# Transposed attention probabilities in the score banks, regrouped attention steps, and three loads moved into the projection

## The chip, the cores and the metric

The kernel runs on one core of a Trainium2 chip. The time is device microseconds of that core for one execution of the whole program, lower is better. Engines: PE multiplies matrices (PEld loads its weights, beside it), DVE, ACT and POOL work on vectors, and SP here only issues transfers. PE writes its results to eight PSUM banks of 128 x 512 float32; ACT and DVE read them from there.

## What is computed

One layer of a hybrid decoder: 2048 tokens of width 1024, all in float32. The parts that matter here are the projection and the two mixers.

```python
proj = h @ w_in[l]
# heads A: causal attention, 8 heads, query blocks of 128 tokens
s = einsum('bqhd,bkhd->bhqk', qn, k_nope) + einsum('bqhr,bkr->bhqk', qp, k_pe)
s = where(k_pos <= q_pos, s * scale, -inf)
p = softmax(s, axis=-1)
o = einsum('bhqk,bkhd->bqhd', p, v)
# heads B: gated delta rule, a recurrence over chunks of tokens, 4 heads
v_new = u_c - einsum('bhcd,bhde->bhce', w_c, state)
o_c = einsum('bhcd,bhde->bhce', q_c, state) + einsum('bhcs,bhse->bhce', a_c, v_new)
state = state * exp(g_last) + einsum('bhcd,bhce->bhde', kd_c, v_new)
x = x + gate_a * (concat([y_mla, y_gdn]) @ w_out[l])
```

After that come a second norm, a mixture of experts and a final norm; neither is touched.

## The kernel before, in words

The program is a row of parts with a barrier between them. `projection` (L73) makes keys, queries, values and the delta rule's inputs, 16 tiles of 128 tokens, and stores them to scratch tensors in HBM (`kn_d`, `kp_d`, `v_d`, `qkv_d`, `g_d`). `mix` (L806) loads them again and runs both mixers at once. `output`, `routing`, `experts` and `finish` follow.

Within a part each engine runs one list of instructions in order, and semaphores keep the engines apart. In `projection` the list `order` (L77) is written out by hand; SP runs through it and issues a store wherever a step has one (L227 to L261).

In `mix` the list comes from a planner, `mix_order` (L707). It has two streams. The delta stream is a fixed row of steps for each chunk of 128 tokens (K and KA make products of keys, VT and KD transpose, KS and QS read the state, TR, DS and AV update it, Y and WU combine inverted blocks, I is a piece of POOL's inversion, M a piece of the modulation). The attention stream is cut into 80 units, called quads: a quad is a query tile, four heads and up to four key tiles (its width, 1 to 4), and its steps are

- S: eight score matmuls into four banks of their own, `pS[0..3]`, one for each head (L1453 to L1468). It waits until all four exponentials of the quad before are done.
- X, for each of four heads: DVE takes the row minimum of the score bank (L1321, or L1318 with the mask), ACT takes the exponential into `prob` in SBUF (L1212).
- T, for each of four heads: up to four PE transposes of `prob` (L1469 to L1474) into a bank taken from a pool of three that all delta steps share, then a copy to `probT` in SBUF, by ACT for heads 0 and 2 (L1218), by DVE for heads 1 and 3 (L1326).
- V, for each of two head pairs: the products with the values (L1475 to L1488), and a copy of them by ACT (L1224).
- O, A, AS, B, BX, B2: the parts of a query tile are weighted and put together.

The eight banks are so: four for scores, one for V's output (`pO`), three in the pool (`NBANK`, L811). The planner hands the pool out in the order of the steps (L894 to L913): a step that takes a bank waits on PE until the last reader of that bank is done (L1372). K and KS take two of the three.

Each attention step has a cost in the planner, and a step is put in when the delta steps so far have earned it: `atoms.append((0.13 * n, [("T", j, e)]))` says that each T costs 0.13 per key tile, so delta steps may stand between one T and the next. The delta steps cost 0 to 1.0, and one unit of them earns a fixed number of attention units, so that both streams end together.

At the start of `mix` SP issues its first loads in this order (L1018 to L1031): `kqv` of chunk 0, g of chunk 0, queries of tile 0 (two), the first four tiles of keys (four transfers of `kp_d`, one of `kn_d`), `kqv` and g of chunk 1, values of the first four tiles, and more. PE's first steps are K of chunk 0 and 1 and S of quad 0. DVE can't write K's second product before the first has been stored to `a_d`, and POOL's inversion starts when both have been stored and loaded back (`load_blocks`, L962).

## Time and profile before

| | |
|---|---|
| median of 3 runs | 2556.26 us (2554.1 to 2560.18) |
| the profiled execution | 2557.7 us, its span 2556.0 us |
| PE busy | 2246.4 us, 88% |
| mean granted PE clock | 0.939 |
| projection | to about 690 us |
| mix | about 691 to 1598 us |
| output and after | to 2556 us |

How to read it: times in the trace are microseconds from the start of the span. A PE row's duration is stretched where the granted clock is low, so PE's busy time holds both work and lost clock; idle PE time stands in brackets before the row that ended it, with what released it. Rows of the same kind that touch are merged and counted (x8).

### The profile page before, as it was taken

Reading aid. Unit: us, or ns where it says so; the run is one execution under the profiler, and the core shown is the slowest. Engines: PE = TensorE matmul, PEld = TensorE weight load, DVE = VectorE, ACT = ScalarE, POOL = GpSimd, SP = SyncE. Lnnn points to the kernel's source line nnn. Section 1 sums busy time; section 2 is a strip of 40 time slices with the busy share of each in tenths; the row PEclk is TensorE's granted clock in tenths of the full one; section 3 lists DMA queues with packets and bytes.
Section 4 is the critical chain, followed back from the end, with each engine's and each line's share of the span. In section 5 each row is a group of like instructions: output and inputs, shape, how many; then the busy total and the mean of one; then the engine's idle time right before and its main releaser. Section 6 shows DMA issues by size and latency. Waiting matters only on the chain. (4 is left out here: it accounts for less than half of the span.)

```text
span 2556.0 us, 35821 instructions
## 1 busy us (share of the span) xinstructions
PE 2246.4 (88%) x11478; PEld 1261.6 (49%) x11479; DVE 1034.5 (40%) x2278; ACT 842.9 (33%) x2027; POOL 644.9 (25%) x1119
## 2 busy tenths in 40 slices
PE   6999999999777888888889888799975999999990
PEld 2545545455344555556555565355543444444440
DVE  2434334333344565556556565223444222222223
ACT  2263462633643444444444454111110101010112
POOL 1000000000152532524514420223321222222224
PEclk9999999999887999899989999799987999999995
DMA  9112121111343234324323224733321879999787
GB/s 346 68 62 71 52 79 54 52 54 36 127 147 106 69 108 162 88 80 134 93 96 113 84 71 168 254 120 132 118 80 42 238 204 303 278 323 308 219 237 287
DMA packets 221899, 361.79 MB, mean 142 GB/s; under 512 B 45580, under 2 KB 143527, under 8 KB 218295
## 3 DMA queue, kind: packets, MB, share of 16 engines
q1 hardware_dynamic: 207926, 309.57, 35.5%
q0 software_dynamic: 13824, 50.34, 8.1%
q8 instruction: 82, 1.34, 0.2%
q14 instruction: 67, 0.54, 0.1%
HBM read 259.93 MB, written 99.93 MB: 141 GB/s over the span
## 5 line engine op out<-in xcount | busy, mean ns | idle before, releaser
L687 PE MATMUL pV<-mod_rows_then_work,w_in_sb 128*128 128x512 f32 x768 | 340.1, 596 | 4.1 <-DVE mod_rows_then_work L501 4.1
L2118 PE MATMUL hidden_ps<-w,keys_values_then_all 128*128 x752 | 332.3, 595 | 0.1
L1212 ACT ACTIVATE probs<-scores,neg_max 128x512 f32<-128x512 f32 (+3 forms) x320 | 198.6, 624 | 337.5 <-DVE neg_max L1321 216.1
L1473 PE MATMUL bank<-ident,probs 128*128 128x128 f32 x1088 | 181.4, 299 | 112.3 <-ACT probs_T L1218 68.2
L2118 PEld LDWEIGHTS hidden_ps<-w,keys_values_then_all 128*128 128x128 f32 x752 | 143.5, 191 | 181.1 <-issue 181.0
L687 PEld LDWEIGHTS pV<-mod_rows_then_work,w_in_sb 128*128 128x128 f32 x768 | 144.4, 191 | 177.0 <-issue 176.2
L1767 PE MATMUL out_ps<-keys_values_then_all 128*128 128x512 f32 x512 | 227.3, 602 | 2.5 <-ACT keys_values_then_all L1632 2.5
L1473 PEld LDWEIGHTS bank<-ident,probs 128*128 128x128 f32 x1088 | 126.2, 149 | 156.9 <-ACT probs_T L1218 84.1
L2128 PE MATMUL expert_ps<-w_sb,keys_values_then_all 128*128 x368 | 169.8, 604 | 0.0
L2048 ACT ACTIVATE keys_values_then_all<-hidden_ps 128x256 f32<-128x256 f32 x47 | 18.1, 385 | 455.3 <-PE hidden_ps L2118 455.3
L1767 PEld LDWEIGHTS out_ps<-keys_values_then_all 128*128 128x128 f32 x512 | 97.4, 193 | 122.7 <-issue 117.4
L1326 DVE COPY probs_T<-bank 128x512 f32<-128x512 f32 (+3 forms) x160 | 97.4, 609 | 142.8 <-PE bank L1473 142.2
L1321 DVE TENSOR_REDUCE neg_max<-scores 128x1 f32<-128x512 f32 x192 | 122.7, 684 | 74.1 <-PE scores L1465 73.6
L1465 PE MATMUL scores<-keys_values_then_all,queries 64*128 64x512 f32 (+3 forms) x640 | 150.6, 593 | 0.0
L1125 POOL TENSOR_TENSOR keys_values_then_all<-keys_values_then_all 32x31 f32<-32x31 f32 (+15 forms) x248 | 121.0, 488 | 115.5 <-DMA keys_values_then_all<-a_d 95.6
L1486 PE MATMUL outT_ps<-probs_T,keys_values_then_all 128*64 128x128 f32 x2176 | 146.9, 282 | 0.0
L1127 POOL TENSOR_TENSOR keys_values_then_all<-keys_values_then_all 32x31 f32<-32x31 f32 (+15 forms) x248 | 133.2, 537 | 19.4
L1486 PEld LDWEIGHTS outT_ps<-probs_T,keys_values_then_all 128*64 128x64 f32 x2176 | 119.8, 139 | 36.5 <-issue 32.8
L2077 DVE TENSOR_TENSOR keys_values_then_all<-keys_values_then_all,hidden_ps 128x256 f32<-128x256 f32 x47 | 19.8, 421 | 277.2 <-ACT keys_values_then_all L2048 277.2
L2013 POOL DMA_INDIRECT x_d<-keys_values_then_all,out_row x46 | 73.3, 1594 | 185.9 <-DVE keys_values_then_all L2086 173.0
L2086 DVE SCALAR_TENSOR_TENSOR keys_values_then_all<-expert_ps,slot_gate,keys_values_then_all 128x512 f32<-128x512 f32 x92 | 64.8, 747 | 133.1 <-PE expert_ps L2128 133.1
L632 PE MATMUL pG<-w_in_sb,mod_rows_then_work 128*128 128x512 f32 x256 | 114.5, 601 | 0.0
(355 smaller groups left out, 3233.1 us busy)
## 6 DMA issues: line engine op xcount, KB each, us to landing
w<-in_w_dram SPq DMA_DIRECT2D x64, 1024.0 KB
w_sb<-in_w_dram SPq DMA_DIRECT2D x32, 1024.0 KB
w_mod_rows<-in_w_mod_dram SPq DMA_DIRECT2D x16, 1024.0 KB, 4.8
kqv<-qkv_d SPq DMA_DIRECT2D x16, 768.0 KB, 4.9
mod_rows_then_work<-in_w_mod_dram SPq DMA_DIRECT2D x4, 2048.0 KB, 14.9
x_in<-in_x_dram SPq DMA_DIRECT2D x16, 512.0 KB, 5.1
qkv_d<-l_out SPq DMA_DIRECT2D x32, 256.0 KB, 2.3
keys_values_then_all<-y_d SPq DMA_DIRECT2D x16, 512.0 KB, 4.7
```

The costliest lines, as they stand in the source:

```text
L632: last = pe.matmul(pG[:], hT[:, n // ST % 2, k, n % ST * P:(n % ST + 1) * P], win[:, k, GATE0:GATE0 + GH * GD], start=(k == 0), stop=(k == ...
L687: last = pe.matmul(pV[n % 2][:], win[:, k, QKV0 + c * P:QKV0 + (c + 1) * P], hT[:, s % 2, k, :], start=(k == 0), stop=(k == ND - 1))
L1125: then(pool.tensor_tensor(prod, Ab[:, j, j + 1:].unsqueeze(2).to_broadcast([n, below, upto]), Tb[:, j:j + 1, 0:upto].to_broadcast([n, belo ...
L1127: then(pool.tensor_tensor(Tb[:, j + 1:, 0:upto], Tb[:, j + 1:, 0:upto], prod, ALU.subtract))
L1212: act.activation(prob[:, e, 0:w].rearrange("p t k -> p (t k)"), pS[e][:, 0:w * P], ACT.Exp, scale=-1.0, bias=nmin[:, i % 2, h, b:b + 1], a ...
L1321: dve.tensor_reduce(nmin[:, i % 2, h, b:b + 1], pS[e][:, 0:w], AX.X, ALU.min).then_inc(min_ready, 1)
L1465: last = pe.matmul(pS[e][:, 0:w * P], qN[row64[e % 2], i % 2, hp], kN[row64[e % 2], 4 * b:4 * b + w, hp], start=False, stop=True)
L1473: last = pe.transpose(bank[b0][:, t], prob[:, e, t], m.ident[:])
L1486: last = pe.matmul(pO[64 * e:64 * e + 64, step[2]], v[:, 4 * b + t, h * DV:(h + 1) * DV], probT[:, 2 * step[2] + e, t], start=(t == 0), st ...
L1767: last = pe.matmul(pX[:, half], yT[par][:, k], wo[:, k, half * 512:(half + 1) * 512], start=(k == 0), stop=(k == ND - 1))
L2118: last = pe.matmul(pH[par][:], xT[par][:, k], m.w13[:, ds(slot, 1), k].rearrange("p s n -> p (s n)"), start=(k == 0), stop=(k == ND - 1))
L2128: last = pe.matmul(pY[:, half], hT[par][:, k], m.w2b[:, ds(slot, 1), k, half * 512:(half + 1) * 512].rearrange("p s n -> p (s n)"), start= ...
```

## The change

Four things change.

1. The transposes of head e go into `pS[e]`, the bank from which its exponential was just read, and the copies read from there. T leaves the list of steps that take a bank from the pool (`uses`). S of the next quad no longer waits for the exponentials but for the copies of the quad before (`t_copied`, both halves).
2. The planner's attention steps are grouped otherwise: T of heads 0 and 1 are one piece with 0.2 per key tile, T of heads 2 and 3 one piece with 0.05, then the O steps, then S with 0.8 (was 0.66), then V of both pairs and X of heads 2 and 3 as one piece with 0.65, in the order V, X, X, V (was V, X, V, X in two pieces). The sum is as before, 1.7. The small steps A and AS move ahead of the last V for some tiles.
3. The first four key tiles, the first four value tiles and `kqv` of chunk 0 are loaded near the end of the projection: SP issues them (seven transfers) after the HQ step of tile 13. The three groups of loads are gone from the start of `mix`.
4. For that the big buffer `m.kv` is allocated before the projection, which works inside it: its rows, weights and scratch are laid out there so that the places of the first keys, values and `kqv` are free by then. The rows for the decay move from half 0 to half 1 of `x_in`, with a wait for one more tile. Keys lie in four segments (`KEYS`) with two views each.

```diff
-        big = sb("mod_rows_then_work", [P, 2, ND, D])
-        flat = big[:].rearrange("p a k n -> p (a k n)")
+        flat = m.kv[:, 0:KV_W]
+        space = Arena(m.kv, (KV_W, KV_N))
         mod_rows = flat.rearrange("p (k n) -> p k n", k=ND)
         QKV0, GATE0 = LOWW, LOWW + NC * P
-        wuq, wukv = sb("w_uq_sb", [P, 2, AH * QK]), sb("w_ukv_sb", [P, AH * (NOPE + DV)])
-        xin, xn = sb("x_in", [P, 2, D]), sb("x_normed", [P, D])
+        xn, xin = space([P, D]), space([P, 2, D])
+        wuq, wukv = space([P, 2, AH * QK]), space([P, AH * (NOPE + DV)])
...
-        gate = sb("gate_out", [P, GH * GD])
+        gate = space([P, GH * GD])
...
-        alog, dtb = xin[:, 0, 0:GH], xin[:, 0, GH:2 * GH]
-        xs, absx, bcl, alpha = (xin[:, 0, at:at + NT * GH] for at in (64, 128, 192, 256))
+        alog, dtb = xin[:, 1, 0:GH], xin[:, 1, GH:2 * GH]
+        xs, absx, bcl, alpha = (xin[:, 1, at:at + NT * GH] for at in (64, 128, 192, 256))
...
+            def load_first():
+                wait(conv_proj, 3 * NC)
+                for i in range(2):
+                    wait(out_stored[i], 16 * NL // 2)
+                    wait(vt_stored[i], 16 * GH // 2)
+                sp.dma_start(first_kqv(m), m.qkv_d[0:1].rearrange("t p c i -> p (t c) i")).then_inc(m.kq0_loaded, 16)
+                wait(kn_stored, 16 * ST)
+                wait(kp_stored, 16 * ST)
+                load_keys(sp, m, 0, m.k0_loaded)
+                wait(xT_ready, NT)
+                wait(xn_written, NT - 1)
+                wait(v_stored, 16 * ST)
+                load_values(sp, m, 0, m.v0_loaded)
...
-                    wait(xn_written, NT - 1)
+                    wait(xn_written, NT)
...
+                    if n == NT - 3:
+                        load_first()
...
-        for e in range(4):
-            atoms.append((0.13 * n, [("T", j, e)]))
-            if i and first and e < 2:
-                atoms.append((0.0, [(("BX", "B2")[e], i - 1, 0)]))
-        if ahead:
-            atoms.append((0.66 * ahead, [("S", j + 1), ("X", j + 1, 0), ("X", j + 1, 1)]))
         o = j - quads.index((i, 0, 0))
+        atoms.append((0.2 * n, [("T", j, 0), ("T", j, 1)] + [("BX", i - 1, 0)] * (i > 0 and first)))
+        atoms.append((0.05 * n, [("T", j, 2), ("T", j, 3)] + [("B2", i - 1, 0)] * (i > 0 and first)))
         if i and o < AH // 4:
             for hp in (2 * o, 2 * o + 1):
                 atoms.append((0.13 * (TILE[i - 1] // 4 + 1), [("O", i - 1, hp)]))
-        for p in range(2):
-            atoms.append((0.26 * n, [("V", j, p)] + [("X", j + 1, 2 + p)] * (ahead > 0)))
-        if i and o == AH // 4 - 1:
+        if ahead:
+            atoms.append((0.8 * ahead, [("S", j + 1), ("X", j + 1, 0), ("X", j + 1, 1)]))
+        if i and last:
+            atoms.append((0.0, [("A", i - 1, 0)] * (TILE[i] < 4) + [("AS", i - 1, 0)]))
+        atoms.append((0.65 * n, [("V", j, 0)] + [("X", j + 1, 2), ("X", j + 1, 3)] * (ahead > 0) + [("V", j, 1)]))
+        if i and o == AH // 4 - 1 and TILE[i] >= 4:
...
+KEYS = [(2048, 0)] + [(10240 + 512 * s, 4096 + 2048 * s) for s in range(3)]
+KQ0, CORNER = 2560, 11776
...
+def load_keys(sp, m, s, loaded):
+    kP, kN = key_views(m, s)
+    for r in range(4):
+        sp.dma_start(kP[r * ROPE:(r + 1) * ROPE], m.kp_d[4 * s * ROPE:4 * (s + 1) * ROPE, :].rearrange("(t p) k -> p t k", p=ROPE)
+                     ).then_inc(loaded, 16)
+    sp.dma_start(kN.rearrange("p t b k -> p t (b k)"), m.kn_d[4 * s * P:4 * (s + 1) * P, :].rearrange("(t p) n -> p t n", p=P)
+                 ).then_inc(loaded, 16)
+
+
+def load_values(sp, m, s, loaded):
+    sp.dma_start(m.kv[:, KV_W + s * 4 * AH * DV:KV_W + (s + 1) * 4 * AH * DV].rearrange("p (t n) -> p t n", t=4),
+                 m.v_d[4 * s * P:4 * (s + 1) * P, :].rearrange("(t p) n -> p t n", p=P)).then_inc(loaded, 16)
...
-        kq = [sb(f"kqv{i}", [P, NC, P]) for i in range(2)]
+        kq = [first_kqv(m), sb("kqv1", [P, NC, P])[:]]
...
-        uses = {"K": 2, "VT": 1, "KD": 1, "KS": 2, "Y": 1, "WU": 1, "TR": 1, "DS": 1, "AV": 1, "M": 1, "T": 1, "O": 1}
+        uses = {"K": 2, "VT": 1, "KD": 1, "KS": 2, "Y": 1, "WU": 1, "TR": 1, "DS": 1, "AV": 1, "M": 1, "O": 1}
...
-                    "T": [(t_copied[lv % 2], 2 * n + lv // 2 + 1)], "O": [(part_ready, n * (AH // 2) + lv + 1)]}[kind]
+                    "DS": [(state_ready, n + 1)], "AV": [(o_ready, n + 1)], "M": [(mod_added, n + 1)], "O": [(part_ready, n * (AH // 2) + lv + 1)]}[kind]
...
-            load_kq(0)
...
-            load_k(0)
...
-            load_v(0)
...
-                            load_k(s)
-                            load_v(s)
+                            load_keys(sp, m, s, k_loaded[s])
+                            load_values(sp, m, s, v_loaded[s])
...
-                    act.copy(probT[:, e, 0:w], bank[at_bank[step][0]][:, 0:w]).then_inc(t_copied[0], 1)
+                    act.copy(probT[:, e, 0:w].rearrange("p t q -> p (t q)"), pS[e][:, 0:w * P]).then_inc(t_copied[0], 1)
...
-                    dve.tensor_copy(probT[:, e, 0:w], bank[at_bank[step][0]][:, 0:w]).then_inc(t_copied[1], 1)
+                    dve.tensor_copy(probT[:, e, 0:w].rearrange("p t q -> p (t q)"), pS[e][:, 0:w * P]).then_inc(t_copied[1], 1)
...
-                    wait(exp_done, 4 * n)
+                    for half in range(2):
+                        wait(t_copied[half], 2 * n)
...
-                        last = pe.transpose(bank[b0][:, t], prob[:, e, t], m.ident[:])
+                        last = pe.transpose(pS[e][:, t * P:(t + 1) * P], prob[:, e, t], m.ident[:])
...
+        m.kv = sb("keys_values_then_all", [P, KV_N])
+        m.k0_loaded, m.v0_loaded, m.kq0_loaded = (ctx.enter_context(nc.semaphore(n)) for n in ("k0_loaded", "v0_loaded", "kq0_loaded"))
```

## Rows read from the trace of the kernel before

**Rows 1.** The page, costliest groups: the transposes, whole span (count, busy, mean ns, idle before).

```profile
L1473 PE MATMUL bank<-ident,probs 128*128 128x128 f32 x1088 | 181.4, 299 | 112.3 <-ACT probs_T L1218 68.2
```

**Rows 2.** Stages: start:end us, length, busy of PE, PEld, DVE, ACT, POOL, clock, DMA share.

```profile
680.00:740.00 60.00, 33.78 (x224) 20.05 (x224) 23.95 (x84) 19.91 (x58) 19.01 (x38) 0.74 0.66 225
740.00:800.00 60.00, 40.14 (x258) 25.71 (x259) 23.14 (x81) 22.50 (x74) 25.76 (x46) 0.77 0.11 38
801.00:1594.00 793.00, 681.78 (x6139) 456.70 (x6131) 469.79 (x1095) 360.86 (x1020) 286.38 (x520) 0.94 0.34 108
```

**Rows 3.** The largest group of PE in 801:1594: count, busy us, mean ns, idle before.

```profile
L1473 PE MATMUL bank<-ident,probs 128*128 128x128 f32 x992 | 160.7, 296 | 86.5 <-ACT probs_T L1218 50.7 <-ACT v_new L1198 7.2 <-DVE probs_T L1326 6.4
```

**Rows 4.** PE's waits in 801:1594: instruction, releaser, total us, times, longest us.

```profile
PE bank L1473 <- ACT probs_T L1218: 50.7, 37, 4.1
PE bank L1473 <- ACT probs L1212: 5.4, 4, 2.7
```

**Rows 5.** PE in order of time: start us, us, instruction, count, idle before it and releaser.

```profile
1200.74 1.97 PE L1383 MATMUL bank<-keys_queries_ahead 128*128 128x256 f32 x8 [1.00 <-issue]
1202.54 0.60 PE L1473 MATMUL bank<-ident,probs 128*128 128x128 f32 x4
1203.81 0.66 PE L1473 MATMUL bank<-ident,probs 128*128 128x128 f32 x4 [0.68 <-ACT probs_T L1218]
1204.40 1.14 PE L1462 MATMUL scores<-keys_values_then_all,rope_queries 32*128 32x512 f32 x8
1205.47 1.99 PE L1465 MATMUL scores<-keys_values_then_all,queries 64*128 64x512 f32 x8
...
1214.27 1.25 PE L1473 MATMUL bank<-ident,probs 128*128 128x128 f32 x8 [0.69 <-DVE v_then_residual L1272]
1215.46 1.13 PE L1462 MATMUL scores<-keys_values_then_all,rope_queries 32*128 32x512 f32 x6
```

**Rows 6.** ACT in the same stretch.

```profile
1199.37 0.70 ACT L1212 ACTIVATE probs<-scores,neg_max 128x512 f32<-128x512 f32 x1
1203.17 0.59 ACT L1218 COPY probs_T<-bank 128x512 f32<-128x512 f32 x1 [2.54 <-PE bank L1473]
...
1211.02 0.69 ACT L1212 ACTIVATE probs<-scores,neg_max 128x512 f32<-128x512 f32 x1
```

**Rows 7.** Last exponential and next S: the first and last of 69 quads.

```profile
805.79 0.71 ACT L1212 ACTIVATE probs<-scores,neg_max 128x512 f32<-128x512 f32 x1
812.07 1.24 PE L1462 MATMUL scores<-keys_values_then_all,rope_queries 32*128 32x256 f32 x8
...
1568.41 0.59 ACT L1212 ACTIVATE probs<-scores,neg_max 128x384 f32<-128x384 f32 x1
1573.88 0.93 PE L1462 MATMUL scores<-keys_values_then_all,rope_queries 32*128 32x384 f32 x8
```

**Rows 8.** PE where the second kernel part begins.

```profile
695.39 3.78 PE L1383 MATMUL bank<-kqv 128*128 128x256 f32 x8 [15.63 <-DMA kqv<-qkv_d]
702.34 2.09 PE L1462 MATMUL scores<-keys_values_then_all,rope_queries 32*128 32x512 f32 x8 [3.17 <-DMA keys_values_then_all<-kn_d]
...
716.21 1.12 PE L1473 MATMUL bank<-ident,probs 128*128 128x128 f32 x4 [4.23 <-DVE probs_T L1326]
```

**Rows 9.** Transfers issued by SP: start us, us of the queue, line, what.

```profile
604.65 0.46 SPq L233 DMA_DIRECT2D x_in<-in_dt_bias_dram  x1
613.52 0.33 SPq L239 DMA_DIRECT2D gate_d<-gate_out  x1
...
691.14 0.33 SPq L951 DMA_DIRECT2D kqv<-qkv_d  x1
692.93 2.04 SPq L936 DMA_DIRECT2D keys_values_then_all<-kp_d  x4
703.78 0.42 SPq L958 DMA_DIRECT2D a_d<-A_ahead  x1
714.32 1.48 SPq L967 DMA_DIRECT2D keys_values_then_all<-a_d  x4
```

More of the change, by code:

```diff
@@ L724, in mix_order @@
                 atoms.append((0.13 * (TILE[i - 1] // 4 + 1), [("O", i - 1, hp)]))
-        for p in range(2):
-            atoms.append((0.26 * n, [("V", j, p)] + [("X", j + 1, 2 + p)] * (ahead > 0)))
-        if i and o == AH // 4 - 1:
+        if ahead:
[4 more added lines that the diff above has]
+        if i and o == AH // 4 - 1 and TILE[i] >= 4:
             atoms.append((0.0, [("A", i - 1, 0)]))
-        if i and last:
-            atoms.append((0.0, [("AS", i - 1, 0)]))
         if last:
@@ L846, in mix @@
         modw, mod_sum = sb("w_mod_rows", [P, 2 * D]), sb("mod_sum", [P, 2, 512])
-        kP = m.kv[:, 0:KP_W].rearrange("p (t k) -> p t k", t=NT)
-        kN = m.kv[:, KP_W:KP_W + KN_W].rearrange("p (t b k) -> p t b k", t=NT, b=AH // 2)
+        kP, kN = zip(*(key_views(m, s) for s in range(len(KV) - 1)))
         v = m.kv[:, KV_W:].rearrange("p (t n) -> p t n", t=NT)
@@ L865, in mix @@
         g_loaded = [sem(f"g_loaded{i}") for i in range(2)]
-        kq_loaded, gate_loaded = [sem(f"kq_loaded{i}") for i in range(2)], [sem(f"gate_loaded{i}") for i in range(2)]
+        kq_loaded, gate_loaded = [m.kq0_loaded, sem("kq_loaded1")], [sem(f"gate_loaded{i}") for i in range(2)]
         dm_ready, exp_ready, em_ready = sem("dm_ready"), sem("exp_ready"), sem("em_ready")
@@ L881, in mix @@
             "modw_loaded", "mod_ready", "mod_added", "bias_loaded", "mod_stored", "bias_zero"))
-        k_loaded = [sem(f"k_loaded{s}") for s in range(len(KV) - 1)]
-        v_loaded = [sem(f"v_loaded{s}") for s in range(len(KV) - 1)]
+        k_loaded = [m.k0_loaded] + [sem(f"k_loaded{s}") for s in range(1, len(KV) - 1)]
+        v_loaded = [m.v0_loaded] + [sem(f"v_loaded{s}") for s in range(1, len(KV) - 1)]
         first_use = [min(i for i in range(NT) if TILE[i] >= t) for t in KV[:-1]]
@@ L931, in _ @@
             wait = waiter(sp)
-            def load_k(n):
-                t, end = KV[n], KV[n + 1]
-                for r in range(4):
-                    sp.dma_start(kP[row32[r], t:end], m.kp_d[t * ROPE:end * ROPE, :].rearrange("(t p) k -> p t k", p=ROPE)
-                                 ).then_inc(k_loaded[n], 16)
-                sp.dma_start(kN[:, t:end].rearrange("p t b k -> p t (b k)"),
-                             m.kn_d[t * P:end * P, :].rearrange("(t p) n -> p t n", p=P)).then_inc(k_loaded[n], 16)
-            def load_v(n):
-                t, end = KV[n], KV[n + 1]
-                sp.dma_start(v[:, t:end], m.v_d[t * P:end * P, :].rearrange("(t p) n -> p t n", p=P)).then_inc(v_loaded[n], 16)
             def load_q(i):
```

22 lines of the change are left out of this document (13 added, 9 removed).

## The prediction, made before the changed kernel was run

> **What bounds the kernel now.** I read the stages first [rows 2]. The change touches the end of the projection and the mixing part, so 801 to 1594 us is the stretch to look at: 793 us in which PE, the busiest engine, is busy for 681.8 us and idle for 111.2 us, at a granted clock of 0.94. DVE is busy for 469.8 us and ACT for 360.9 us, so neither is full. PE bounds it, and what it loses it loses in two ways: idle time, and half-speed clock that comes with it.
>
> Then the groups of PE's instructions: of the 111.2 us idle, 86.5 us stand directly before the transposes T of line 1473 [rows 3]. Over the whole span it is 112.3 us [rows 1], so 25.8 us more lie in the start of the mixing part. The waits say on whom: 50.7 us, 37 times, until ACT had copied an earlier transposed bank to `probT`; only 5.4 us until an exponential was done, the one thing that T really needs [rows 4]. So nearly all of it is a wait for one of the three pool banks.
>
> In order of time one sees why [rows 5]. K at 1200.74 takes two of the three banks and holds them until KA has read them. T of head 2 (1202.54) gets the one that is left, and T of head 3 has to wait until ACT has copied that same bank: 1203.81, with S right behind at 1204.40. ACT had ended the last exponential of this quad at 1199.37 + 0.70 = 1200.07 [rows 6], so S came 4.3 us after it. In the next quad the last exponential ends at 1211.02 + 0.69 = 1211.71 [rows 6] and S starts at 1215.46 [rows 5], 3.75 us after it, now held up by KS, which also takes two banks. I followed 69 quads this way. Their first and last have 5.6 and 4.9 us [rows 7]; the mean is 3.3 us. From S of the quad after the first at 812.07 to the last S at 1573.88 are 68 periods [rows 7], 11.2 us each. Of such a period PE works 86% = 9.6 us and idles 1.6 us.
>
> **The change part by part.**
>
> *Transposes in the score banks.* No PE, ACT or DVE work is removed or added: 16 transposes and four copies of a full quad stay. What goes is the wait for a pool bank. What comes is that S waits for the copies of the quad before. I work out the two limits of a quad that are left.
>
> Limit 1 is PE's work, 9.6 us for each period at today's clock.
>
> Limit 2 is the ring S, minimum, exponential, transpose, copy, S. S takes about 3.1 us (1204.40 to 1205.47 + 1.99 = 1207.46 [rows 5]). The last exponential ends on the mean of the 69 quads 4.9 us after S (4.2 us in the second quad of rows 5 and 6: 1211.71 less 1207.46). Then T of one head, 0.66 us [rows 5], its copy, 0.59 us on ACT [rows 6] and about 0.7 on DVE, and some 0.3 us for the three hand-overs. That is 3.1 + 4.9 + 0.66 + 0.7 + 0.3 = 9.7 us.
>
> So both limits lie near 9.6 to 9.7 us, against 11.2 now. Neither is reached each time: the delta steps are unevenly spread, K and KS still stand on PE between other steps and their readers on DVE, and where two equal limits meet, the worse of the two counts. I take half of today's idle time, 0.8 us, as what stays: 9.6 + 0.8 = 10.4 us. Bounds: nothing stays (9.6), and all of it stays or more (11.2 and above, the rivals).
>
> With less idle time the clock stays up more of the time. I have rows for the clock at two shares of PE: 0.77 where PE is busy for 67% of the time (740 to 800) and 0.94 at 86% [rows 2]; in the projection it is at full speed with PE nearly always busy. 9.6 of 10.4 is 92%, on which I put 0.97. PE's work is then 9.6 x 0.94 / 0.97 = 9.3 us, and the period 10.1 us. Bounds: no gain in clock (10.4), and full clock (9.8).
>
> The stretch becomes 793 x 10.1 / 11.2 = 715 us: **78 us less**, of which 57 are idle time and 21 clock.
>
> *The steps regrouped.* The planner's sum for a quad is unchanged (1.7 for each key tile), so as many quads fall to a chunk as before. T of all four heads now stand together, and the delta steps and the O steps stand behind them, ahead of S: they cover the copies, about 1 us [rows 5, 6]. If that cover is missing (QS and KA have no PE work), S waits for 1 us; this is in the 0.8 us that I leave. X of head 3 is no longer queued on ACT behind V's copy, so the last exponential can end some tenths earlier; DVE's minima still stand behind the delta steps' reads. I cost the two together at nothing, between -0.4 and +0.7 us a quad, since T of head 3 must now come before the delta steps that stand behind it. The moved A and AS steps cost nothing in most quads: they wait on POOL's list, and V and S of PE cover them.
>
> *What stands behind the new wait.* S waits on PE for ACT's and DVE's copies. Queued behind it on PE are all delta steps and V. The copies stand on their engines directly behind the T steps, so nothing of the delta stream is ahead of them but what was already issued.
>
> *The start of the mixing part.* 25.8 us idle before T lie here [rows 1, 3], at a clock of 0.74 to 0.77 [rows 2]. The waits are longer, since DVE's copy at 716.21 stands behind K's product of chunk 1, and that waits for the store of chunk 0 to `a_d` [rows 8]. This part of the wait stays, it only moves to S. I take 10 of the 25.8 us (bounds 0 and 20).
>
> *Loads ahead of the barrier.* Before, PE's first K waits until 695.39 for `kqv`, and S until 702.34 for the keys [rows 8]; SP begins to issue at 691.14 [rows 9]. After, K can start at once, 4 us earlier, and S waits for its queries. Those are now the second and third transfer, and as `kqv` landed 4.2 us after its issue, S can start near 696, some 6 us earlier. What is late next is the store of K's products: SP issues it at 703.78, 1.8 us or so behind what POOL's memsets allow, and its blocks can be loaded only at 714.32, 10.5 us later [rows 9], with 3 MB of keys, values and `kqv` in the same queue. Without these it should be back a few microseconds sooner. I take **6 us** for the whole (bounds 2 and 10).
>
> *Their place in the projection.* Seven transfers more on SP: four of 0.5 us (2.04 for four), three of 0.3 to 0.5 [rows 9], 3.2 us in all. They stand behind the stores of tile 13; there SP has nothing to issue from 605.11 to 613.52 [rows 9]. All that they wait for (products of the third group, x of tile 15, stores of the first tiles) is done by then. PE is busy there all the time and waits for none of this. Cost 0; if the cover were gone, 3.2 us. The wait for one more tile ahead of the decay rows is met by then too: 0.
>
> *The sum.* 78 + 10 + 6 = 94 us. The profiled execution took 2557.7 us, of which its span is 2556.0; 2557.7 - 94 = 2463.7. The median of the runs is 1.4 us under that execution, so I predict 2462 us.
>
> *A rule that speaks against it.* The trace shows that the time before a T is a wait for a bank to be emptied [rows 4]. The Trainium skill says on the page Perfetto Trace Analysis, section Matmuls, that independent groups of matmuls should rotate through different PSUM banks, so that ACT and DVE empty one while PE fills the next. The change gives up this rotation for the transposes: scores and transposes of a head share one bank, and S can't start while the copy reads. By the rule the ring above would be the longer limit, which is the first rival.
>
> **The rivals.**
>
> 1. *The ring becomes the bound, slower.* S waits for copies that come late, because ACT's two copies stand behind the last exponential and DVE's second behind the small steps of BX and B2. For: ACT is also the one for whom T waits now, 50.7 us [rows 4]. Against: 3.3 us pass today between the last exponential and the next S, and the ring needs 1.7 of them. It decides from 3.3 us on; at 4.0 us, each of 69 quads is 0.7 us longer: +48, less the 16 us of the start: 2556 + 32 = 2588 us.
> 2. *The exponential is the real bound, half the gain.* Most waits for ACT's copy end shortly after the last exponential, as that copy stands behind it on ACT. If denser work on DVE and ACT (59% and 46% busy now [rows 2], 66% and 50% then) pushes the last exponential 0.8 us out, the period is 10.8 us: 28 us less, with the start 44 and no clock: 2512 us.
> 3. *All idle time goes.* Period 9.6 x 0.94 / 0.99 + 0.3 = 9.4 us, 127 us less, with the start 143: 2413 us. Against: delta steps have waits of their own, 24.7 us in the stretch (111.2 - 86.5) [rows 2, 3].
> 4. *The clock falls.* T are now four in a row, 16 transposes, a quarter of PE's work in the stretch (160.7 of 681.8 us [rows 2, 3]). If PE counts as less active in them and the clock falls to 0.90, PE's work is 10.0 us, the period 10.8: 28 us less: 2512 us. The rows don't show the clock falling on transposes, only behind idle time. The Trainium skill has such a rule (TensorE: Matmul & The Clock Gate, Part 4: PE-mode transpose): transposes don't count as PE being busy.
> 5. *The change doesn't do what it says*: the waits only change their name, and the start is hidden. 2556 us.
>
> **How the numbers follow.** Forecast 0.56 (2435 to 2490: the bounds of clock, start and of 0.5 to 1.1 us idle in a quad); rival 1 0.09; rival 2 0.17; rival 3 0.09; rival 4 0.05; rival 5 0.04. The range leaves out rival 1, rival 5 and the far part of rival 3: 2430 to 2530. About 0.2% of the time (5 us) is what a measurement can tell from no change. Faster 0.87, the same 0.04, slower 0.09.
>
> **What would show it.** Idle before L1473 near 20 us or less instead of 112.3, released by exponentials; a new wait of S (L1462) on the copies, under 1 us a quad; the pool's steps with hardly a wait for `probs_T`; the clock near 0.97 in the stretch; S to S 10.1 us; PE's first K near 691.3 and the first S near 696; the projection's end unmoved. The prediction is wrong if S or T wait for over 1.6 us a quad together, or if the last exponential ends much later than 4.9 us after S.

## The result, and the profile after

The changed kernel takes **2448.93 us** (median of 4 runs, 2446.39 to 2452.07), the kernel before on the same chip 2557.57 us (2554.1 to 2560.18). The ratio of the two (the time after divided by the time before, as everywhere below) is 0.9577, with a 95% interval of 0.956 to 0.9594: 109 us less. The profiled execution took 2449.63 us, its span 2447.9 us, at a mean granted clock of 0.955. Forecast were 2462 us, in a range of 2430 to 2530.

First the transposes T, as a group over the whole span (count, busy, mean ns, idle before); it answers to [rows 1]:

```profile
L1496 PE MATMUL scores<-ident,probs 128*128 128x128 f32 x1088 | 156.5, 286 | 38.3 <-ACT probs L1234 37.6
```

The idle time before them fell from 112.3 to 38.3 us, and what ends it is no longer a copy but an exponential, which T really needs. Then the stages (start:end us, length, busy of PE, PEld, DVE, ACT, POOL, clock, DMA share, GB/s), against [rows 2]; the last row is the stretch from S of quad 11 to S of quad 79, the same work as 812.07 to 1573.88 before:

```profile
680.00:740.00 60.00, 35.98 (x241) 22.03 (x240) 27.03 (x95) 22.95 (x70) 23.56 (x46) 0.77 0.54 177
740.00:800.00 60.00, 48.24 (x395) 30.98 (x394) 33.92 (x108) 27.18 (x90) 23.68 (x42) 0.89 0.34 100
790.19:1469.61 679.42, 617.77 (x5984) 432.26 (x5985) 450.74 (x1052) 345.25 (x991) 285.57 (x517) 0.98 0.36 112
```

And PE's waits from 690 to 1500 us (instruction, releaser, total us, times, longest us), against [rows 4]. Two lines are the new wait of S for the copies, 22.3 us in all:

```profile
PE scores L1496 <- ACT probs L1234: 37.6, 26, 6.7
PE scores L1485 <- DVE probs_T L1348: 14.9, 18, 5.5
...
PE scores L1485 <- ACT probs_T L1240: 7.4, 10, 1.2
```

In order of time this is the stretch of [rows 5] in the changed kernel, with the step K that held two of three pool banks:

```profile
1139.28 1.09 PE L1496 MATMUL scores<-ident,probs 128*128 128x128 f32 x8
1140.21 1.89 PE L1405 MATMUL bank<-keys_queries_ahead 128*128 128x256 f32 x8
1141.94 1.04 PE L1496 MATMUL scores<-ident,probs 128*128 128x128 f32 x8
1144.01 1.14 PE L1485 MATMUL scores<-keys_values_then_all,rope_queries 32*128 32x512 f32 x8 [1.03 <-DVE probs_T L1348]
```

T of heads 2 and 3 follow K at once, where head 3 had to wait before. Here S stands directly behind T and waits 1.03 us for DVE's copy.

**Where the 108.1 us of the span went** (starts of the first S and of S of quads 11 and 79 in both traces; the quads are numbered from 0): the first S comes 5.5 us earlier (702.34, now 696.80); from there to quad 11 it is 16.3 us less; from quad 11 to 79, 82.4 us less (761.8, now 679.4); from there to the last O step of the mixing part 4.8 us less; behind it nothing that counts (about 1 us more).

### The profile page after: what moved, and what is told of

Same layout as the page of the kernel before. It is cut to its first block and busy times, and to the rows that moved or that the text cites. A ratio compares the mean times of both kernels' runs of the same rounds, so it can differ in the third digit from the quotient of the medians.

```text
span 2447.9 us, 35572 instructions
## 1 busy us (share of the span) xinstructions
PE 2191.6 (90%) x11478; PEld 1245.6 (51%) x11479; DVE 1034.5 (42%) x2278; ACT 835.2 (34%) x2027; POOL 646.8 (26%) x1119
## 5 line engine op out<-in xcount | busy, mean ns | idle before, releaser
L704 PE MATMUL pV<-keys_values_then_all,w_in_sb 128*128 128x512 f32 x768 | 340.1, 596 | 4.1 <-DVE keys_values_then_all L518 4.1
L704 PEld LDWEIGHTS pV<-keys_values_then_all,w_in_sb 128*128 128x128 f32 x768 | 144.4, 191 | 177.0 <-issue 176.2
L1496 PE MATMUL scores<-ident,probs 128*128 128x128 f32 x1088 | 156.5, 286 | 38.3 <-ACT probs L1234 37.6
L1496 PEld LDWEIGHTS scores<-ident,probs 128*128 128x128 f32 x1088 | 121.0, 144 | 67.8 <-ACT probs L1234 59.3
L1147 POOL TENSOR_TENSOR keys_values_then_all<-keys_values_then_all 32x31 f32<-32x31 f32 (+15 forms) x248 | 121.3, 489 | 101.0 <-DMA keys_values_then_all<-a_d 81.0
L1488 PE MATMUL scores<-keys_values_then_all,queries 64*128 64x512 f32 (+3 forms) x640 | 143.6, 569 | 0.0
L1149 POOL TENSOR_TENSOR keys_values_then_all<-keys_values_then_all 32x31 f32<-32x31 f32 (+15 forms) x248 | 133.5, 538 | 19.4
L1509 PE MATMUL outT_ps<-probs_T,keys_values_then_all 128*64 128x128 f32 x2176 | 138.2, 278 | 0.0
L1348 DVE COPY probs_T<-scores 128x512 f32<-128x512 f32 (+3 forms) x160 | 96.9, 610 | 97.3 <-PE scores L1496 96.5
L2036 POOL DMA_INDIRECT x_d<-keys_values_then_all,out_row x46 | 73.3, 1594 | 185.9 <-DVE keys_values_then_all L2109 173.0
L649 PE MATMUL pG<-w_in_sb,keys_values_then_all 128*128 128x512 f32 x256 | 114.6, 601 | 0.0
```

The costliest lines, as they stand in the source:

```text
L649: last = pe.matmul(pG[:], hT[:, n // ST % 2, k, n % ST * P:(n % ST + 1) * P], win[:, k, GATE0:GATE0 + GH * GD], start=(k == 0), stop=(k == ...
L704: last = pe.matmul(pV[n % 2][:], win[:, k, QKV0 + c * P:QKV0 + (c + 1) * P], hT[:, s % 2, k, :], start=(k == 0), stop=(k == ND - 1))
L1147: then(pool.tensor_tensor(prod, Ab[:, j, j + 1:].unsqueeze(2).to_broadcast([n, below, upto]), Tb[:, j:j + 1, 0:upto].to_broadcast([n, belo ...
L1149: then(pool.tensor_tensor(Tb[:, j + 1:, 0:upto], Tb[:, j + 1:, 0:upto], prod, ALU.subtract))
L1488: last = pe.matmul(pS[e][:, 0:w * P], qN[row64[e % 2], i % 2, hp], kN[b][row64[e % 2], 0:w, hp], start=False, stop=True)
L1496: last = pe.transpose(pS[e][:, t * P:(t + 1) * P], prob[:, e, t], m.ident[:])
```

## The experiments

All ratios are against the kernel before, run on the same chip beside each. Where microseconds of two kernels are compared, they are the distance of their ratios times 2557 us; the intervals make each such number uncertain by 3 to 7 us.

**The three parts alone.** The transposes in the score banks, with the whole planner part (all pieces and weights) and the loads of before (banks_only):

```diff
-        atoms.append((0.2 * n, [("T", j, 0), ("T", j, 1)] + ...
+        for e in range(4):
+            atoms.append((0.13 * n, [("T", j, e)]))
...
-                    if n == NT - 3:
-                        load_first()
```

> Only the first part of the change: transposes in the score banks, S waiting for the copies; the steps ordered as before, the first loads at the start of mixing. If the wait for a pool bank was the cause, the idle time before the transposes falls from 112 us to under 40, and the time to about 2480 us (some 75 us less), a little worse than with the regrouped steps, since S stands directly behind the last transpose and its wait for the copies (about 1 us a quad) is not covered. If the regrouping is what brings the gain, it stays above 2540 us.

Measured: 2505.27 us, ratio 0.9801 (0.9785 to 0.9817), 51 us less. The waits of PE from 690 to 1545 us:

```profile
PE scores L1475 <- DVE probs_T L1338: 55.7, 38, 6.0
PE scores L1486 <- ACT probs L1224: 33.3, 45, 2.9
...
PE scores L1475 <- ACT probs_T L1230: 12.0, 11, 1.7
```

T no longer waits for a bank, and the idle time before it fell to 33.9 us, as expected. But S now waits 67.7 us for copies, three times as long as in the full change, and the time misses the expected 2480 us by 25 us: the missing cover costs far more than "a little".

The new grouping alone, with T in the pool, S behind the exponentials and the loads of before (grouping_only):

```diff
-        uses = {..., "M": 1, "O": 1}
+        uses = {..., "M": 1, "T": 1, "O": 1}
...
-                    for half in range(2):
-                        wait(t_copied[half], 2 * n)
+                    wait(exp_done, 4 * n)
...
-                        last = pe.transpose(pS[e][:, t * P:(t + 1) * P], ...
+                        last = pe.transpose(bank[b0][:, t], ...
```

> Only the second part: the steps regrouped as in the change, transposes still in the three pool banks, S waiting for the exponentials, the first loads at the start of mixing. By the theory of the pool banks this brings nothing or costs: four transposes in a row find three banks at most, so 2550 to 2580 us. By the rival (the order is what counts) it is near 2470 us.

Measured: 2549.11 us, ratio 0.9971 (0.9959 to 0.9982), 7 us less; it costs nothing, and the rival's 2470 us are far off. From 690 to 1600 us:

```profile
PE bank L1483 <- ACT probs_T L1228: 61.9, 65, 6.4
PE bank L1483 <- ACT probs L1222: 23.0, 19, 7.2
PE bank L1483 <- DVE probs_T L1336: 12.5, 15, 4.5
```

Four transposes in a row need four turns of three pool banks, and so T waits for copies as before (74.4 us here, 80.3 in the kernel before, over its mixing part).

The loads alone (loads_only: both edits above taken back, the loads kept), and the full change without them (late_loads):

> Only the loads (and the buffer laid out anew): first keys, values and kqv loaded during the projection, transposes and order as before. Expected 6 us less than before (2 to 10), with the first S near 696 us instead of 702. If the later chain at the start hides it: no change, under 2 us. If the clock of the start profits too: 10 to 15 us less.

Measured: 2552.39 us, ratio 0.9976 (0.9966 to 0.9986), 6 us less; its first S stands at 696.63 us.

> The change without the loads: they are issued at the start of mixing as before. If the parts add up, it is 5 to 8 us slower than the changed kernel (2449), so about 2455 us; if the start hides them, 2449; if they are worth more together with the new banks, over 2460.

Measured: 2453.6 us, ratio 0.9593 (0.9577 to 0.9609), 104 us less; first S at 701.24 us. The loads are worth 4 to 6 us (the 4 are within the noise) and add up with the rest as far as the intervals tell. The other two parts don't: 51 and 7 us apart, 104 together. **46 us, give or take some 6, come only from the two at once**, and the prediction had put the regrouping at nothing.

**Why the grouping pays only with the new banks.** On PE, S stands directly behind the last T in 29 of 79 quads before and in 9 after, and all four T stand in a row in 39 of 80 quads before and in 74 after. (These are the steps with work for PE. The counts of the expectation below, 12, 2 and 44, are of the planner's whole list, in which steps without work for PE stand between T and S too.) So I moved the delta steps between T and S to ahead of T; S then stands directly behind T in 45 quads (s_behind_t):

```diff
-        atoms.append((0.2 * n, [("T", j, 0), ("T", j, 1)] + ...
+        atoms.append((0.95 * n, [("T", j, 0), ("T", j, 1)] + ...
...
-            atoms.append((0.8 * ahead, [("S", j + 1), ...
+            atoms.append((0.05 * ahead, [("S", j + 1), ...
```

> The changed kernel with two weights of its planner moved: the pair T of heads 0 and 1 gets 0.95 per tile (was 0.2), S gets 0.05 (was 0.8). In 44 of 79 quads S then stands directly behind the last transpose, where in the changed kernel a step of the delta layer stands between them (directly behind in 2, in 12 in the old order). Banks, loads and the order within each piece are those of the changed kernel. Theory (the score bank of head 3 is free for S only when its transposes are copied out, and the new grouping pays because it puts a delta step under that copy): S waits 50 us or more on copies in the stretch (13 in the changed kernel, 49 with the new banks in the old order), the transposes wait a little less on the exponentials, time 2475 to 2495. Rival (the distance from T to S does nothing; what counts is that the four transposes stand in one row and both last exponentials in one piece): 2445 to 2457, the waits of S rise by less than 15 us.

Measured: 2485.61 us, ratio 0.9722 (0.9699 to 0.9746): 37 us of the gain are gone. PE's waits from 690 to 1530 us:

```profile
PE scores L1485 <- DVE probs_T L1348: 45.4, 44, 5.6
PE scores L1485 <- ACT probs_T L1240: 18.9, 16, 2.2
PE scores L1496 <- ACT probs L1234: 17.0, 15, 2.6
```

S waits 64.3 us on copies, about as long as in the kernel with the banks alone, against 22.3 us. The rival, that the distance does nothing, has fallen. Not all of the 37 us need be this wait: T waits 20.6 us less for exponentials here, and some 18 us more stand before M and O steps (12.3 and 11.3 us, in the changed kernel 2.8 and 2.3). Why these grew was not followed. With T in the score banks a delta or O step should stand between T and S; with T in the pool, S needs no copy, and the whole grouping, this distance with it, bought 7 us.

**The order V, X, X, V**, which on ACT takes X of head 3 out from behind the copy of V (taken back in v_x_v_x):

```diff
-        atoms.append((0.65 * n, [("V", j, 0)] + [("X", j + 1, 2), ("X", j + 1, 3)] * (ahead > 0) + [("V", j, 1)]))
+        atoms.append((0.65 * n, [("V", j, 0)] + [("X", j + 1, 2)] * (ahead > 0) + [("V", j, 1)] + [("X", j + 1, 3)] * (ahead > 0)))
```

> The changed kernel with the order V, X, V, X inside the last piece of each quad (the changed kernel has V, X, X, V): on ScalarE the exponential of head 3 again stands behind the copy that the second V needs. Theory A (this order is why the last exponential ends 4.1 us after S instead of 4.8, and the saved 0.7 us is on the ring of S, exponentials, transposes): last exponential at 4.8 us again, and as the ring is only partly the bound, 0.2 to 0.4 us a quad, 2465 to 2480. Theory B (the transposes are rarely waiting for head 3 at all, since a delta step stands ahead of them): last exponential at 4.8 us, time within 5 us of 2449.

Measured: 2465.47 us, ratio 0.9641 (0.9621 to 0.966), 16 us of the gain gone, as theory A gave it (at the lower end of its range). Its account was only half right: the last exponential ends on the mean 4.4 us after S, not 4.8 (4.1 in the changed kernel), so 0.3 us of the 0.7 come from this order and the rest from elsewhere in the grouping. The waits of T on the exponentials are not much longer but far more frequent (26 times and 37.6 us in the changed kernel), so small tenths count in many quads. With the 37 us of s_behind_t this makes 53, which is what the grouping is worth beside the banks (104 less 51); that the two simply add is not shown:

```profile
PE scores L1496 <- ACT probs L1234: 46.5, 62, 6.7
```

**Whose pool wait it was.** T goes into the score banks and waits for no pool bank, but still takes its turn in the rotation, so that the delta steps wait for T's copies (slot_kept):

```diff
-        uses = {..., "M": 1, "O": 1}
+        uses = {..., "M": 1, "T": 1, "O": 1}
...
+                    "T": [(t_copied[lv % 2], 2 * n + lv // 2 + 1)], "O": ...
...
-                released[b] = q
+                released[b] = [x for x in (released[b] or []) if kind == "T"] + [q]
...
-                for q, value in bank_free.get(step, []):
+                for q, value in bank_free.get(step, []) if kind != "T" else []:
```

> The changed kernel, in which the transposes go into the score banks and do not wait for the pool, but the planner's rotation still gives them a turn: the step that gets that bank next waits for the copies out of the score bank, as it did in the old rotation. So the transposes are freed and the delta steps are not. Theory (the gain of the banks is the transposes' own wait; what the delta steps gain from a freer pool is little): 2447 to 2458. Rival (a good part is that the K, VT, KS, Y, DS and M steps find a bank free earlier): 2465 to 2490, with waits of 15 us and more on the copies at the delta steps' first matmuls.

Measured: 2473.88 us, ratio 0.9679 (0.9658 to 0.97). My theory missed: 26 us of the gain need the turn that is free for the other steps, not only T's own freedom. The profiled execution was the shortest of the five, 2465.39 us, so its rows show less than the 26 us. The waits of pool steps on T's copies (eleven lines, 19.2 us in all from 690 to 1515 us; the first four):

```profile
PE bank L1456 <- ACT probs_T L1241: 4.7, 5, 1.3
PE bank L1517 <- DVE probs_T L1349: 4.5, 6, 1.0
...
PE bank L1517 <- ACT probs_T L1241: 2.4, 5, 0.9
...
PE bank L1422 <- ACT probs_T L1241: 1.7, 2, 1.1
```

In the changed kernel there are none; in the one before the pool steps other than T waited 12.7 us on T's copies over the mixing part, and T did most of the waiting.

**What is left: is it S?** S waits for all four copies, though its first matmul needs the first bank alone (split_waits):

```diff
-                    for half in range(2):
-                        wait(t_copied[half], 2 * n)
                     for e in range(4):
+                        wait(t_copied[e % 2], 2 * (n - 1) + e // 2 + 1)
```

> The changed kernel, in which the first matmul of S on bank e waits only for the copy of head e of the quad before, and no longer for all four copies. S waited 22 us on copies in the changed kernel from 690 to 1500 us (the copy of head 3 in most of them). Theory (what S waits for is the last copy, and three matmuls of 0.5 to 0.6 us each fit ahead of bank 3): most of the 22 us go, half of it comes back as waits of the transposes behind, 2434 to 2442. Rival (TensorE loses nothing there, because the same time is then spent waiting for the exponentials): 2446 to 2451.

Measured: 2447.48 us, ratio 0.9578 (0.9557 to 0.9599): nothing gained, as the rival had it. From 690 to 1500 us S's waits fell to 7.4 us:

```profile
PE scores L1495 <- ACT probs L1234: 38.3, 24, 6.8
...
PE scores L1484 <- DVE probs_T L1348: 4.3, 1, 4.3
...
PE scores L1484 <- ACT probs_T L1240: 3.1, 6, 0.7
```

but S, begun 0.18 us sooner after the copies on the mean of 69 quads, also takes 0.16 us longer (3.00 against 2.84), which fits a last matmul that still has to wait for the last copy. T's wait on the exponentials is what it was.

**Or is it what the exponentials stand behind?** The longest waits of T are few. Around one of them in the changed kernel, DVE, POOL and PE (start, us, instruction, idle before):

```profile
918.67 1.13 DVE L1275 SCALAR_TENSOR_TENSOR A_ahead<-bank,beta,decay 128x128 f32<-128x128 f32 x4 [3.48 <-issue]
919.72 1.28 DVE L1343 TENSOR_REDUCE neg_max<-scores 128x1 f32<-128x512 f32 x2
```
```profile
916.57 0.67 POOL L1149 TENSOR_TENSOR keys_values_then_all<-keys_values_then_all 32x252 f32<-32x252 f32 x1
917.32 1.26 POOL L1161 TENSOR_TENSOR decay<-g_rows_then_decay,upper 128x512 f32<-128x512 f32 x1
```
```profile
921.26 1.97 PE L1496 MATMUL scores<-ident,probs 128*128 128x128 f32 x8 [4.59 <-ACT probs L1234]
```

POOL makes the decay at 917.32, behind a row of pieces of the inversion (L1147, L1149); DVE's product of the keys needs it and starts at 918.67; the minima of the quad stand behind that product, then the exponentials, then T. So I moved the step that makes the decay ahead (early_g):

```diff
-        body = [(0.8, ("Y", n, 1))] * prep
+        body = [(0.0, ("G", d))] * (d < NT)
+        body += [(0.8, ("Y", n, 1))] * prep
...
-        late += [(0.0, ("G", d))] * (d < NT)
```

> The changed kernel with step G (the decay of a coming chunk, on GpSimd and VectorE) issued at the start of the turn's body, not near its end behind the pieces of the inversion. In the profile of the changed kernel the three longest waits of the transposes for exponentials (4 to 7 us each) come where VectorE's product of the keys waits for a decay that GpSimd makes late, and the row minima of the next quad stand behind that product. Theory (that queue causes the long waits): the waits of 4 us and more go, the transposes' wait for exponentials falls from 38 to some 22 us, 2433 to 2442. Rival (they come from something else, or G only displaces other work of GpSimd by as much): 2445 to 2455.

Measured: 2433.77 us, ratio 0.9512 (0.9491 to 0.9534), 17 us faster than the changed kernel. POOL, then DVE and PE at the same place:

```profile
895.62 1.28 POOL L1161 TENSOR_TENSOR decay<-g_rows_then_decay,upper 128x512 f32<-128x512 f32 x1 [2.53 <-issue]
```
```profile
917.34 1.12 DVE L1275 SCALAR_TENSOR_TENSOR A_ahead<-bank,beta,decay 128x128 f32<-128x128 f32 x4
```
```profile
919.92 1.32 PE L1496 MATMUL scores<-ident,probs 128*128 128x128 f32 x8 [0.85 <-ACT probs L1234]
```

The product no longer waits, and T waits 0.85 us instead of 4.59. T's waits on exponentials fell to 25.7 us in all. The longest, 6.7 us, stayed; it has another owner, in the changed kernel at 755.48 on ACT:

```profile
755.48 0.72 ACT L1256 ACTIVATE attn_y<-attn_out,attn_rstd 128x512 f32<-128x512 f32 x1 [5.34 <-POOL attn_rstd L1184]
756.11 0.67 ACT L1234 ACTIVATE probs<-scores,neg_max 128x512 f32<-128x512 f32 x1
```

The change had moved step AS ahead of the last V, and with it ahead of the exponentials of heads 2 and 3; the prediction costed that at nothing. On top of early_g, AS was put back behind the piece with V (as_late):

```diff
-            atoms.append((0.0, [("A", i - 1, 0)] * (TILE[i] < 4) + [("AS", i - 1, 0)]))
+            atoms.append((0.0, [("A", i - 1, 0)] * (TILE[i] < 4)))
...
+        if i and last:
+            atoms.append((0.0, [("AS", i - 1, 0)]))
```

> The kernel early_g with one step moved more: AS (ScalarE scales the attention rows of the tile before by attn_rstd, which GpSimd makes) behind the last V of a tile's last quad, where the changed kernel put it ahead of that V and so ahead of the exponentials of heads 2 and 3. In the changed kernel AS waits 8.5 us in three places for attn_rstd, 5.34 us of it at 750 us, where GpSimd works off the pieces of the inversion first; the exponential of head 3 there ends 9.3 us after S, and the transposes wait 6.7 us. Theory (that wait of AS is what holds the exponentials): the wait of 6.7 us goes to under 2, 2426 to 2431. Rival (the wait at 750 us is made up behind it, or AS stands in the way of the copies of V instead): 2432 to 2440.

Measured: **2427.57 us, ratio 0.9504** (0.9484 to 0.9525), 2 us better than early_g by the ratios and 6 by the medians; the intervals overlap, so the gain in time is not settled. The effect on the queue is: the longest wait of T on exponentials is gone, with 12.4 us left in all, while AS still waits, now behind all four exponentials:

```profile
PE scores L1498 <- ACT probs L1236: 12.4, 20, 1.5
```
```profile
745.90 0.69 ACT L1236 ACTIVATE probs<-scores,neg_max 128x512 f32<-128x512 f32 x1
...
750.67 0.72 ACT L1258 ACTIVATE attn_y<-attn_out,attn_rstd 128x512 f32<-128x512 f32 x1 [3.73 <-POOL attn_rstd L1186]
```

A part came back as other waits on PE: K at 753.31 waits 5.7 us for attn_out (1.9 us in early_g), and the last O steps wait 8.8 us for out_T (3.7 us). ACT's copies of T now stand behind AS and start only at 751.29, but K's wait ends later still.

**Does the late decay cost the same before the change?** The move of G alone, in the kernel before (early_g_on_before, the same diff as early_g):

> The kernel before the change, with only step G moved to the start of the turn's body, as in early_g. Theory (the late decay costs its 3 to 6 us at two or three quads whatever the banks are, since the row minima stand behind it on VectorE in both kernels): 2538 to 2548, a gain of 9 to 18 us as behind the change. Rival (in the kernel before, the transposes are held by the pool at these places too, so that the earlier exponentials find no earlier transposes and the queue only became a bound with the change): 2550 to 2559.

Measured: 2546.52 us, ratio 0.9948 (0.9935 to 0.9961), 13 us less, against 17 behind the change. So this queue costs about the same with either use of the banks; it was no part of what the change did.

The edit on S's waits on top of as_late:

> The kernel as_late and the edit of split_waits on top (S's first matmul on a bank waits for that head's copy alone). In as_late the S steps wait 27 us on copies and the transposes only 12 us on exponentials, where behind split_waits alone they waited 38. Theory (the edit bought nothing before because the exponentials were next; with their long waits gone a part of the time stays won): 2418 to 2425. Rival (S is drawn out inside instead, its last matmul still waits for the last copy, and the exponentials of the last head start when they did): 2426 to 2430.

Measured: 2431.2 us, ratio 0.9497 (0.9483 to 0.9512), the same as as_late within the intervals; the theory (2418 to 2425 us) missed. The split of the waits buys nothing here either. Both are faster than the changed kernel, by 19 to 20 us by the ratios.

## Why the prediction was right, point by point

- **What bounds** (PE, with 86.5 us of its idle time before T, a wait for pool banks): right. The waits on copies before T went, and the time with them.
- **The period** of a quad: forecast 10.1 us, measured 679.42 / 68 = 9.99 (11.20 before). Of it PE works 617.77 / 68 = 9.08 us (forecast 9.3) and idles 0.91 (forecast 0.8 before the gain in clock). These 68 periods gave 82.4 us, where 78 were forecast for a slightly longer stretch (793 us, the periods are 762 of it).
- **Its two terms were mis-sized, in opposite ways.** Forecast were 57 us from idle time and 21 from the clock. Over the same work PE's idle time fell from 102 to 61.7 us, 40 us; PE's busy time from 659.9 to 617.8 us, 42 us. That 40 and 42 make nearly the sum of 57 and 21 is luck: the two errors cancelled. The clock rose to 0.98, not 0.97; 9.70 x (1 - 0.94 / 0.98) = 0.40 us a quad is 27 of the 42 us (20 to 33, as the clocks are read to two digits). The other 15 or so are not explained by the mean clock. V shows that there is such a rest: the same 1936 instructions took 279 and 277 ns each, but cover 128.4 us before and 121.6 after, so they overlap more with their neighbours. That gaps ahead of an instruction cost this overlap is argued, not shown.
- **Limit 2, the ring.** The forecast put it at 9.7 us and S's new wait under 1 us a quad. S's waits are 22.3 us over 79 quads, 0.3 us each. On the mean S takes 2.84 us, the last exponential ends 4.13 us behind it, T of head 3 starts 0.65 us later, it and the last copy take 1.37 us, and S follows after 0.97 us. These make 9.96 us, the period, since they divide it without a rest; the sum doesn't show that the ring is closed. T starts within 0.35 us of the last exponential in 35 of 69 quads, S within 0.15 us of the last copy in 27, both in 11: only there the ring is closed, and elsewhere PE has other work at one of the two places. The last exponential comes 4.1 us after S, not 4.9; the order V, X, X, V gives 0.3 of that.
- **The regrouping at nothing**: the one step that failed. Alone it is worth 7 us, with the banks some 53 (104 less 51). The prediction saw the mechanism (the steps behind T "cover the copies, about 1 us") and did not charge the other side: that without the regrouping S would wait for the copies (67.7 us in banks_only; the prediction had left 1 us a quad for it, inside its 0.8 us of idle time). The sum came out since it was made for both parts at once; the credit belongs to the two together.
- **"The pool's steps with hardly a wait"**: right, and worth more than thought: 26 us come from the freed turn.
- **A and AS at nothing**: right in most quads, wrong at one, where ACT waits 5.3 us up to 755.48 and T 6.7 us; what that costs in time is not settled (as_late).
- **The start**: forecast 10 us (0 to 20), measured 16.3. The wait that was to stay, moved to S, stayed: DVE's copy stands behind the product of chunk 1, and S waits 5.46 us for it. The difference is PE's busy time. Over the same work, first S to S of quad 11, PE's idle time fell from 31.5 to 22.6 us, 8.9 us as against the forecast 10, and its busy time by 7.4 us at a clock of 0.84 instead of 0.80, which had not been counted. Before and after, and then PE at the start after the change:

```profile
702.34:812.07 109.73, 78.24 (x516) 47.39 (x516) 46.63 (x163) 41.64 (x136) 42.15 (x78) 0.80 0.35 117
696.80:790.19 93.39, 70.84 (x521) 44.71 (x521) 48.70 (x168) 40.64 (x137) 46.24 (x84) 0.84 0.38 121
```
```profile
691.77 3.60 PE L1405 MATMUL bank<-keys_values_then_all 128*128 128x256 f32 x8 [11.76 <-PEq L103]
696.80 1.14 PE L1485 MATMUL scores<-keys_values_then_all,rope_queries 32*128 32x512 f32 x8 [1.43 <-DMA queries<-qn_d]
...
711.29 2.09 PE L1485 MATMUL scores<-keys_values_then_all,rope_queries 32*128 32x512 f32 x8 [5.46 <-DVE probs_T L1348]
```

- **The loads**: forecast 6 us, first K 691.3, first S 696. Measured 4 and 6 us, 691.77 and 696.80, the latter released by its queries, as forecast. The store of K's products is issued at 702.45 instead of 703.78, and its blocks are loaded from 708.72 instead of 714.32. These answer to [rows 9]:

```profile
604.58 0.32 SPq L204 DMA_DIRECT2D keys_values_then_all<-qkv_d  x1
605.00 1.82 SPq L817 DMA_DIRECT2D keys_values_then_all<-kp_d  x4
...
613.77 0.33 SPq L254 DMA_DIRECT2D gate_d<-keys_values_then_all  x1
...
702.45 0.42 SPq L983 DMA_DIRECT2D a_d<-A_ahead  x1
...
708.72 1.48 SPq L992 DMA_DIRECT2D keys_values_then_all<-a_d  x4
```

- **Their place in the projection at nothing**: right. They sit in the gap of SP, the next store is at 613.77 (613.52 before), and the projection's last PE instruction starts at 679.74 us (679.49 before).
- **The rivals.** The slower ring did not come: from the last exponential to the next S 2.99 us pass, below the 3.3 at which it would decide. (Before, the mean over the 69 quads was 3.36 us, which the prediction gives as 3.3.) The exponential as the real bound, with half the gain: not so either, since the exponentials came sooner, not later; yet what T still waits for is the exponentials, and removing their causes gave the next 17 us. Not all idle time went. The clock did not fall with four T in a row: it is 0.98 in the stretch, and T's mean went from 295 to 284 ns.
- **Two rules of the Trainium skill.** By the Trainium skill (Perfetto Trace Analysis, section Matmuls) independent groups of matmuls should rotate through different PSUM banks. The rotation that was given up cost T 80 us of waits, and the reuse of a head's own bank costs S 22 us, or 64 to 68 us in the kernels where S stands directly behind T in 29 or 45 quads instead of 9. So the rule's reason holds here (S does wait for the emptying), but following it was the slower way in a pool of three banks. By the Trainium skill (TensorE: Matmul & The Clock Gate, Part 4: PE-mode transpose) transposes don't count as PE being busy. The trace shows no drop in the granted clock with them. It is no test of the rule, though: at most 16 stand in a row, and eight T take 1.04 to 1.09 us (1139.28 and 1141.94 above), like eight products of the same shape (1.16 and 1.06 us at 1149.92 and 1150.91), so no row tells that they ran in the mode that the rule means.

## What to carry to other kernels

A buffer that a step needs anyway, like the score bank of which only the exponentials were wanted, can serve for the next step and free a turn in a shared pool; the pool's other users may gain from that too (26 of the 109 us here). Such a reuse moves the wait to the buffer's next writer: put independent work between the last use and that writer in the same change, and cost the two together, since here one alone gave half of the gain and the other nearly nothing. Then look for the longest single waits rather than the largest sum: two of them led through DVE or ACT to a step late in POOL's queue, and moving one of these steps in the planner gave 17 us more.

## What the runs showed of the hardware

When PE's idle time fell, its busy time fell too. In the same work the idle time fell by 40 us and PE's busy time by 42, with the granted clock going from 0.94 to 0.98. Over the kernels of this study, from S of quad 11 to S of quad 79 (length, then busy of PE; the clock stands behind POOL's busy time): the kernel with the banks alone, the one with S behind T, and early_g:

```profile
803.89:1523.18 719.29, 639.66 (x5980) 437.21 (x5981) 447.88 (x1051) 349.07 (x991) 283.86 (x517) 0.95 0.34 106
```
```profile
787.24:1508.40 721.16, 626.20 (x5984) 434.95 (x5985) 448.70 (x1052) 345.72 (x991) 286.53 (x517) 0.96 0.34 107
```
```profile
791.95:1456.35 664.40, 612.37 (x5984) 426.51 (x5984) 449.00 (x1052) 345.08 (x991) 284.33 (x517) 0.99 0.36 115
```

Idle time is 79.6, 95.0 and 52.0 us, and the clock is not a function of it alone: the second has more idle time than the first, in fewer and longer gaps (75 against 81, the longest 7.5 against 6.0 us), and yet a higher clock and 13 us less busy time. What decides between them was not tried.

Nor is the busy time a function of the clock alone. These are slot_kept and split_waits, with the changed kernel's clock of 0.98:

```profile
789.79:1489.79 700.00, 625.69 (x5986) 430.93 (x5985) 450.53 (x1053) 345.69 (x991) 284.38 (x517) 0.98 0.35 110
788.77:1467.42 678.65, 626.74 (x5985) 438.42 (x5984) 449.50 (x1054) 345.43 (x992) 285.64 (x517) 0.98 0.36 113
```

Slot_kept has 12.7 us more idle time than the changed kernel (74.3 against 61.7, in 90 gaps against 63) and 7.9 us more busy time: here more idle time went with more busy time at the same clock; why is not shown. Split_waits has 9.7 us less idle time and 9.0 us more busy time, and its stretch is as long as that of the changed kernel: S takes 0.16 us longer in each of 69 quads, 11 us in all, so its wait seems only to have moved inside its rows, where it counts as busy. So a fall in idle time is a gain only when the stretch gets shorter with it.
